# Two attention mixers: narrowed pieces and maxima end at the diagonal (128 columns in place of 256)

## What is computed

```python
# first block, "fox", per block i of 128 queries
s = jnp.einsum('bhqd,bhkd->bhqk', qb, kh) + Fb[..., None] - F[:, :, None, :]
s = jnp.where(kpos[None, :] <= qpos[:, None], s, -jnp.inf)
p = jax.nn.softmax(s, axis=-1)
return jnp.einsum('bhqk,bhkd->bhqd', p, vh)
...
# second block, "mla", per block of 128 queries
s = (jnp.einsum('bqhd,bkhd->bhqk', q_nope[:, q0:q1], k_nope[:, :q1])
     + jnp.einsum('bqhd,bkd->bhqk', q_rope[:, q0:q1], k_rope[:, :q1])).astype(jnp.float32) * scale
s = jnp.where(k_chunk[None, :] <= q_chunk[:, None], s, -jnp.inf)
prob = jax.nn.softmax(s, axis=-1).astype(v.dtype)
outs.append(jnp.einsum('bhqk,bkhd->bqhd', prob, v[:, :q1]))
```

## Time and profile before

| | us |
|---|---|
| median of 3 runs | 2282.21 (2280.11 to 2282.62) |
| span of the profiled execution | 2284.0 |
| TensorE busy | 2128.9 (93%), 9840 matmuls |
| TensorE weight loads busy | 1691.4 (74%) |
| VectorE busy | 1125.8 (49%) |
| GpSimd busy | 1105.4 (48%) |
| ScalarE busy | 671.8 (29%) |
| DMA, mean | 47 GB/s |
| mean granted TensorE clock | 0.964 of 2.4 GHz |

### The profile page before, as it was taken

How to read it: one execution, slowest core, us unless ns; L and a number is a source line. 1 busy time by engine, 2 the same in 40 slices (tenths; PEclk the granted TensorE clock), 3 DMA queues, 4 the chain that set the end, 5 groups by cost and what they waited for, 6 DMA issues and landing times.

```text
span 2284.0 us, 27160 instructions
## 1 busy us (share of the span) xinstructions
PE 2128.9 (93%) x9840; PEld 1691.4 (74%) x9840; DVE 1125.8 (49%) x1213; ACT 671.8 (29%) x1069; POOL 1105.4 (48%) x657
## 2 busy tenths in 40 slices
PE   5999999988999999999999998998999999989996
PEld 3777776877778878788878876886776777668774
DVE  6545653737541211212111287215777777754576
ACT  3334444221121000000001132114555555560322
POOL 1635554522833634633444383334656666653373
PEclk9999998997999999999999998998999999989998
DMA  3100000112211211211111131110000000001122
GB/s 139 48 19 20 14 14 19 46 38 92 92 46 53 67 55 46 74 46 54 57 55 46 55 101 37 46 46 28 20 19 19 19 19 19 19 28 46 46 69 97
DMA packets 31624, 106.98 MB, mean 47 GB/s; under 512 B 3440, under 2 KB 3632, under 8 KB 31568
## 3 DMA queue, kind: packets, MB, share of 16 engines
q1 hardware_dynamic: 27520, 96.53, 12.7%
q10 hardware_dynamic: 4048, 9.67, 1.2%
HBM read 101.83 MB, written 4.26 MB: 46 GB/s over the span
## 4 chain that ended last, share of the span: by engine, by line
PE 59%; POOL 15%; issue 14%; DVE 8%; ACT 2%; ACTq 0%; POOLq 0%; DMA 0%; DVEq 0%
PE ps L220 45%; POOL probs_lo L677 11%; PE ps L385 4%; PE ps L249 3%; PE ps L237 2%; POOL w_lo L1921 2%; POOL w_hi L1919 2%; DVE h_lo L366 1%; DVE tmp L1747 1%; DVE x L1749 1%; DVE S_all L1287 1%; DVE tmp L362 1%; DVE result L1753 0%; PE ps L1594 0%; DVE ssq L413 0%
## 5 line engine op out<-in xcount | busy, mean ns | idle before, releaser
L1919 POOL TENSOR_TENSOR w_hi<-w_raw,zero 128x1024 fp32r<-128x1024 f32 (+1 forms) x173 | 334.7, 1935 | 816.0 <-PE ps L220 575.7
L1921 POOL TENSOR_TENSOR w_lo<-w_raw,w_hi 128x1024 fp32r<-128x1024 f32 (+1 forms) x173 | 433.0, 2503 | 13.6
L220 PE MATMUL ps<-h_hi,w_lo 128*128 128x512 f32 x1328 | 338.4, 398 | 5.6 <-DVE x L512 5.1
L220 PE MATMUL ps<-h_hi,w_hi 128*128 128x512 f32 x1328 | 328.0, 389 | 0.0
L677 POOL TENSOR_TENSOR probs_lo<-probs,mla_p_hi 128x512 fp32r<-128x512 f32 x192 | 220.3, 1167 | 182.0 <-ACT probs L670 181.9
L220 PE MATMUL ps<-h_lo,w_hi 128*128 128x512 f32 x1216 | 302.0, 391 | 0.0
L220 PEld LDWEIGHTS ps<-h_hi,w_lo 128*128 128x128 f32 x1328 | 251.2, 191 | 61.6 <-issue 10.0
L220 PEld LDWEIGHTS ps<-h_hi,w_hi 128*128 128x128 f32 x1328 | 249.3, 188 | 51.7
L220 PEld LDWEIGHTS ps<-h_lo,w_hi 128*128 128x128 f32 x1216 | 230.0, 189 | 48.4
L1369 DVE TENSOR_TENSOR tmp<-ps,tmp 128x1024 f32<-128x1024 f32 x22 | 26.9, 1224 | 370.3 <-PE ps L220 363.6
L712 DVE TENSOR_REDUCE mx<-ps 128x1 f32<-128x256 f32 (+1 forms) x192 | 144.5, 785 | 78.5 <-PE ps L655 77.8
(11 more groups left out here) (345 smaller groups left out, 3911.7 us busy)
## 6 DMA issues: line engine op xcount, KB each, us to landing
w_raw<-in_wpack SPq DMA_DIRECT2D x173, 512.0 KB, 3.3
x<-in_xT ACTq DMA_DIRECT2D x16, 512.0 KB, 8.3
out<-result SPq DMA_DIRECT2D x8, 512.0 KB, 2.9
p_raw<-in_pT ACTq DMA_DIRECT2D x1, 1024.0 KB, 7.2
const_stage<-in_consts SPq DMA_DIRECT2D x1, 788.0 KB, 4.4
pos_i<-in_pos SPq DMA_DIRECT2D x1, 512.0 KB, 6.4
vec<-in_vecs SPq DMA_DIRECT2D x1, 284.0 KB, 5.3
mla_q_hi<-c_neg ACTq DMA_DIRECT2D x16, 4.0 KB
```

The source lines that it names most:

```text
L220: last = nc.tensor.matmul(dst[:, half, :], w[slot][:, kt, :], a[:, i, t], start=(n == 0), stop=(n == total - 1))
L1919: nc.gpsimd.tensor_tensor(w_hi[s][:, kts, :], raw[s][:, kts, :], no_change[:, kts, :], ALU.add).then_inc(w_hi_done, 1)
L1921: nc.gpsimd.tensor_tensor(w_lo[s][:, kts, :], raw[s][:, kts, :], w_hi[s][:, kts, :].bitcast(F32), ALU.subtract)\
```

## The change

`off` of a piece is no longer held at 256, and neither is the width of a maximum. Two of twelve pieces of every head (3 and 11) become 128 columns wide in place of 256, in everything that is made of them: three score matmuls and the mask, three value matmuls, two exponentials, one subtraction. Two of eight maxima (0 and 4) lose 128 columns in L654, in their mask L655 and in the reduction (256 to 128, and 768 to 640). The order of the instructions on every engine, their number, and all waits stay as they are.

```diff
         for half in range(2):
             for j in range(4 * (half + 1)):
                 d = j * P - half * HALF
-                PIECES.append((half, j, min(max(d, 0), 256), d))
+                PIECES.append((half, j, max(d, 0), d))
...
         def max_width(i):
 
-            w = max(256, (i % 4 + 1) * P)
+            w = (i % 4 + 1) * P
             return w, i // 4 * HALF + w
```

## The result

The changed kernel takes 2255.02 us (median of 4 runs, 2253.48 to 2258.68), the kernel before beside it 2282.41 us (2280.11 to 2283.28): a ratio of 0.9878, interval 0.986 to 0.9897, or 27.4 us less. The profiled execution shows the same, 2284.0 against 2256.9 us of span. From the page of the changed kernel: the span, the busy time of each engine, and the chain's shares.

What follows compares the result with a forecast made beforehand. Bound: a path through TensorE, ScalarE and VectorE, not TensorE alone. An mla step gains 0.51 us; mla 7.6, fox 4.0 and tails 0.8 sum to 12.4 us, forecast 2270 us, range 2261 to 2291.

Steps and rivals of the forecast that it cites:

- What a narrow matmul costs: fp32r matmuls at 128 columns: 0.06 us less only where the next weight load is short (L608, L654, L622).
- L606, L607, L623 and L629 still 0.12: Sign in the profile after: these narrowed matmuls keep 0.12 us, while L622 and L608 take 0.06.
- Rival one: TensorE: columns alone count, every narrowed fp32r matmul 0.06 us less; 18.4 us gained, 2264 us; chance 0.11.
- Rival three: TensorE: fp32r matmuls under 256 columns stream slower, 0.11 us more each; 12 us slower, 2294 us; chance 0.17.
- Score 3: TensorE's score of piece 3: L608 0.06 us less, mask's end 0.05 sooner; together 0.11 us a step.
- the exponentials of piece 3: ScalarE's two exponentials of piece 3: 0.21 us less a step, bounds 0.1 and 0.23.
- reduction 4: VectorE, behind the norm and ahead of maximum 6: 128 fewer columns, 0.13 us less a step.
- Rival two: Only engines other than TensorE gain, ScalarE's 0.21 us ending in another wait; 4 us gained, 2278 us; chance 0.14.
- The four norm instructions on this path: VectorE, between reduction 3 and reduction 4: counted as part of the path through a step, no gain assigned.
- The end of the step: Value 10 and 11, piece 11's exponentials and subtraction: no gain; only L608 in piece 11's score gives 0.06 us.
- L660's wait grows to 1.1 us: TensorE's wait at the end of a step, for the negated maxima: from 0.69 to about 1.1 us.
- The clock: Half-clock steps cost 1.6 us each; count left as is, 3 us either way on the range.

Runs made afterwards that it cites:

- groups of 48: Kernel before plus eight groups of 48 fp32r matmuls between fox and mla; 128 stationary columns cost 0.226 us at 512 moving, 0.121 at 256, 0.111 at 128.
- The last experiments: Separate negation dropped, sign changed in the copy out of PSUM: on the kernel before 2261.96 us, on the changed kernel 2241.06 us.
- piece 3 alone: Kernel before with only piece 3 narrowed to 128 columns, piece 11 and the maxima left at 256: 2278.6 us, ratio 0.9984.
- with piece 11: Kernel before with only piece 11 narrowed to 128 columns, piece 3 and the maxima left at 256: 2273.65 us, ratio 0.9943.
- with the maxima: Kernel before with only maxima 0 and 4 narrowed, the pieces left at 256 columns: 2280.15 us, ratio 0.9987.
- TensorE alone: Kernel before with pieces 3 and 11 narrowed only in TensorE's matmuls, ScalarE and GpSimd still at 256, maxima unchanged: 2289.78 us, ratio 1.0029.
- the others alone: Kernel before with ScalarE's exponentials, GpSimd's subtraction and L629 narrowed for pieces 3 and 11, other matmuls and maxima unchanged: 2260.99 us, ratio 0.9908.
- the rope copy moved: Kernel before, 256 columns, with ScalarE's rope copy behind piece 2 in place of piece 3 in mla: 2280.99 us, ratio 0.9996.
- the late negation: Negation moved into the copy out of PSUM: kernel before 2261.96 us; changed kernel 2241.06; changed kernel with the rope copy behind piece 2 also, 2231.74.
- the extra addition: Kernel before with one more 128x112 GpSimd addition between a head's last subtraction and the next weight unit's split: 2279.76 us, ratio 0.9994.

## Why the prediction was right in direction and short in size

**What a narrow matmul costs: right.** A narrowed score with its mask costs 0.07 us less, and so does a narrowed value with its L629: one matmul's share in each and not three, as forecast. The rows put the saving elsewhere than the prediction did (at L606 and not at L608; L623 at 0.06 with 0.17 behind it at L629), so its sign "L606, L607, L623 and L629 still 0.12" is borne out by the sums and not row by row. The groups of 48 measure 0.11 with 128 stationary columns and 0.06 with 64. Rival one (columns alone count) is out, though its 2264 us lies nearer to the result. Rival three is out too; no narrow matmul costs more than a 256-column one, at the same clock.

**Score 3, the exponentials of piece 3, reduction 4: right.** 0.07 and the mask's end, 0.21 (0.68 to 0.47), and 0.13 (946 to 815 ns). Up to the last mask L655, an undisturbed step is 0.49 to 0.56 us shorter, with 0.51 forecast in mla and 0.57 in fox. Rival two, that the exponentials' gain ends in another wait, did not come. The four norm instructions on this path were taken as work, though one of them is half wait, as shown above; the change leaves that as it is, so it cost the sum nothing.

**The end of the step: wrong, and it is the step that failed.** The prediction had "Value 10 and 11, ScalarE's and GpSimd's share of piece 11: nothing. They lie beside reduction 7 and the negation". It took the negation's 1.55 us for work of its own that starts behind reduction 7. In fact they are the rest of a GpSimd instruction. From the last L655 to L660 a step took 3.14 us before. After, it takes 2.59 at the turn and 2.69 to 2.71 away from it, so 0.55 or 0.44 less. In the step of the rows above it is 0.42: the exponentials of piece 11 0.22 (from L668 to L677 0.74 to 0.52), the subtraction 0.15 (from L677 to `w_hi` 0.69 to 0.54), the mask's end 0.05. At the turn the subtraction gives 0.27, as `w_hi` follows it there without a gap; why it doesn't elsewhere the trace doesn't say. Over the 22 steps it is 11.3 us that were put at zero. The last experiments show a second error in the same term: even without the held negation, L660 stands behind the L629 of piece 11 and not behind reduction 7. There was evidence at hand. Eight numbers a partition in 1.55 us is nine times what the same line took in the first head, and in the last step of each block the wait before L660 was missing along with it; and the chain of the page went over GpSimd inside the steps, with 15%, and was put aside for the list of waits, which names L717 as L660's releaser and can't say that L717 itself was held, because its row counts as busy. The forecast that L660's wait grows to 1.1 us was the test for it, and it read 0.73 to 0.86.

**The clock: a term left at zero that was worth 6.4 us in the steps, or 4.5 net.** Each half-clock step costs the 1.6 us that was forecast. The prediction named six fewer and four more as possible, left the number as it was and gave it 3 us of range; it fell by four in the traced execution. Nothing in the forecast tells which way it would go, and the count isn't even a fixed property of a kernel. The kernel with the groups of 48 has the code of before throughout fox and mla, and its trace has four half-clock steps in place of six; the executions of the kernel before in these experiments had mean granted clocks of 0.964 to 0.970, and 2278.8 to 2288.7 us. The first step of each block lost 1.9 of the 6.4 again (mla's went from 29.44 to 29.89 us, with 5.6 us at half clock in place of 2.1). Behind the last fox step more was lost. These are stretches of 3 us, of the kernel before 11 us behind that step's end and of the changed kernel 21 us behind it:

```profile
356.18:359.18 3.00, 3.00 (x15) 2.39 (x14) 0.00 (x0) 2.01 (x4) 1.44 (x2) 0.90 0.00 0
```

```profile
353.44:356.44 3.00, 3.00 (x10) 2.23 (x10) 0.00 (x0) 1.25 (x3) 1.37 (x2) 0.50 0.00 0
```

Before, the clock was at half for some 10 us there and was back by then; after, for some 20 us. Matched matmul by matmul, the changed kernel has fallen back by 4.6 us at the end of that stretch and by 5.4 some 30 us further on. Some 3 us of it come back by the first mla step, where the kernel before has stretches at half clock that the changed one has elsewhere. So the 2.4 us by which the part between fox and mla grew are put down to the clock; no run isolates it.

**The sum.** Of the forecast's 12.4 us, 11.6 were for the steps, and up to the last L655 they came. The end of the step adds 11.3 to that, the clock 6.4 less 1.9: 27.4. Outside the steps 0.3 were lost where 0.8 were forecast as a gain: 27.1, which is the difference of the two spans.

**What stays open.** Half-clock steps numbered 6 in the kernel before and 2 in the changed one; 6 with piece 3 alone, 7 with piece 11, 5 with the maxima, 11 on TensorE alone, 1 on the others alone; 4 with the groups of 48; 9 with the rope copy moved; 0 in the three kernels with the late negation. (The steps with the extra addition are of two kinds and weren't counted.) That the kernels without the wait before L660 had none, their first steps apart, is what three traces show, one execution of each. Why the changed kernel, whose wait is longer than before, had fewer than each of its parts alone was not settled. So how much of the 27 us would remain in another phase isn't known: some 23 us are in the steps at full clock, 4.5 hang on the clock.

## What to carry to other kernels

When a tiny instruction's row is many times longer than its work, look what runs beside it on the other engines (here GpSimd beside VectorE) and whether the two end together; if so, read it as a wait: compare the least and the median of its line. A list of waits goes one step back only; where it names a releaser, ask what held the releaser. A gain of under 0.6 us a step was eaten (TensorE alone) or nearly doubled (the late negation) by the clock of what follows, so count the half-clock stretches in each variant before its parts are added up.

## What was not expected of the hardware

- A VectorE instruction on 128x8 float32 in SBUF takes 0.17 us, or 1.13, 1.55 and 1.93 with a GpSimd instruction of 1.89 us beside it, and ends 0.03 us behind that one; where the recorded starts lay within 0.02 us, it came out either way, all or nothing. The same negation with its input in PSUM took 0.27 in 24 of 24 cases.
- A VectorE multiplication of 64x512 float32 with both inputs in SBUF (L705) takes 0.68 us, or 1.52 to 1.67 when a GpSimd subtraction had begun ahead of it, and ends 0.55 us behind that one.
- The engine so held is shown as busy. The list of waits names no holder, and the chain, where it passes through the negation, goes on to reduction 7 and not to GpSimd.
- While 48 fp32r matmuls of 64 columns ran back to back, the granted clock was 0.73 over 7.1 us, and each cost more (0.149 us) than one of 128 columns just ahead (0.111).
- Across kernels whose steps differ by 0.1 to 1.8 us, one trace of each, the number of half-clock projections went from 0 to 11, up to 18 us at 1.6 us each, which is more than most of the edits gave themselves.
